# Output projection in token tiles of 512, 512, 64 and 512, 304, 272 in place of 364, 362, 362

## What is computed

```python
def _merge(att, h, mo, g_out, w_out):
    hl = _rmsnorm(jax.nn.sigmoid(mo) * h.astype(mo.dtype), g_out)
    lead = att.shape[:-1]
    mixed = jnp.concatenate([att.astype(hl.dtype), hl.reshape(lead + (LSTM_WIDTH,))], axis=-1)
    return mixed @ w_out
...
        xp = xp + _swiglu_half(xp, g_ffn1[l], w1_gate[l], w1_up[l], w1_down[l])
        dp, kp, vp, Cp, n_p, mp = _mix_prompt(xp, rows, *mix_w)
        xp = xp + dp
        xp = xp + _swiglu_half(xp, g_ffn2[l], w2_gate[l], w2_up[l], w2_down[l])
        xp = _rmsnorm(xp, g_final[l])
```

## Time and profile before

| | |
|---|---|
| Runs | 2407.89, 2411.44, 2412.19 us; median 2411.44 |
| Span of the profiled execution | 2406.2 us (its whole time isn't listed) |
| Mean granted clock of PE over the span | 0.961 |
| PE matmuls, weight loads | 2200.4 us (91%), 2126.2 us (88%) |
| DVE, ACT, POOL | 1016.1, 509.3, 155.5 us |
| HBM | 54 GB/s over the span |

### The profile page before, as it was taken

One profiled execution on the slowest core, in us unless ns is written; L12 is line 12 of the kernel. 1 busy time (PEld: TensorE's weight loads), 2 busy tenths in 40 slices (PEclk: granted clock), 3 DMA queues, 4 the chain that ended last, 5 costly groups with the idle time before them and its releaser, 6 DMA issues.

```text
span 2406.2 us, 32473 instructions
## 1 busy us (share of the span) xinstructions
PE 2200.4 (91%) x13110; PEld 2126.2 (88%) x13110; DVE 1016.1 (42%) x1699; ACT 509.3 (21%) x857; POOL 155.5 (6%) x216
## 2 busy tenths in 40 slices
PE   5999999999999978599994667999999999999997
PEld 4999999999999977488883656989999999999997
DVE  4533334343334365544433572263434333434335
ACT  3310011111011133333333451141111101111102
POOL 2100000000000010212220320010000000000000
PEclk8999999999999998799997887999999999999999
DMA  3301111101111012223220632102111011111002
GB/s 110 107 18 52 35 52 52 52 23 47 35 52 44 0 35 60 80 73 92 84 68 16 174 90 44 36 6 101 53 52 52 17 35 52 52 52 52 17 0 83
DMA packets 128003, 129.83 MB, mean 54 GB/s; under 512 B 10628, under 2 KB 115108, under 8 KB 127952
## 3 DMA queue, kind: packets, MB, share of 16 engines
q1 hardware_dynamic: 120224, 109.49, 15.3%
q0 software_dynamic: 7728, 19.65, 2.7%
HBM read 111.50 MB, written 17.55 MB: 54 GB/s over the span
## 4 chain that ended last, share of the span: by engine, by line
PE 51%; issue 34%; DVE 7%; ACT 5%; DMA 2%; POOL 1%; SPq 0%; DVEq 0%; ACTq 0%; POOLq 0%
PE bank L213 15%; PE bank L215 15%; PE bank L214 14%; PE bank L242 2%; ACT SP L843 1%; DVE RM L1121 1%; PE bank L1282 1%; PE bank L1272 1%; PE bank L1291 1%; DMA XIN<-in_x_prompt 1%; DVE SP L1056 1%; DVE WGL L308 1%; DVE YO L1182 0%; ACT L843 0%; DVE RS L248 0%
## 5 line engine op out<-in xcount | busy, mean ns | idle before, releaser
L213 PE MATMUL bank<-HH,WGH 128*128 128x362 f32 (+1 forms) x2856 | 948.4, 332 | 31.1 <-DVE WGL L308 13.2
L215 PE MATMUL bank<-HH,WGL 128*128 128x362 f32 (+1 forms) x2856 | 940.2, 329 | 0.0
L214 PE MATMUL bank<-HL,WGH 128*128 128x362 f32 (+1 forms) x2856 | 938.7, 329 | 0.0
L213 PEld LDWEIGHTS bank<-HH,WGH 128*128 128x128 f32 x2856 | 542.1, 190 | 42.6 <-issue 39.3
L214 PEld LDWEIGHTS bank<-HL,WGH 128*128 128x128 f32 x2856 | 542.3, 190 | 2.0 <-issue 0.5
L215 PEld LDWEIGHTS bank<-HH,WGL 128*128 128x128 f32 x2856 | 541.2, 189 | 0.0
L355 DVE TENSOR_TENSOR AT<-ST,bank 128x364 f32<-128x364 f32 (+1 forms) x132 | 70.2, 532 | 726.7 <-PE bank L215 726.7
L213 PE MATMUL bank<-AH,WDH 128*128 128x362 f32 (+1 forms) x1056 | 348.5, 330 | 9.8 <-DVE X L367 9.8
L215 PE MATMUL bank<-AH,WDL 128*128 128x362 f32 (+1 forms) x1056 | 346.6, 328 | 0.0
L214 PE MATMUL bank<-AL,WDH 128*128 128x362 f32 (+1 forms) x1056 | 345.4, 327 | 0.0
L367 DVE SCALAR_TENSOR_TENSOR X<-bank,X 128x362 f32<-128x362 f32 (+1 forms) x528 | 276.0, 533 | 154.0 <-PE bank L215 152.0
(11 more groups left out here) (221 smaller groups left out, 1460.7 us busy)
## 6 DMA issues: line engine op xcount, KB each, us to landing
RAWG<-in_w_gate SPq DMA_DIRECT2D x22, 1024.0 KB, 5.4
RAWU<-in_w_up SPq DMA_DIRECT2D x22, 1024.0 KB, 7.9
RAWD<-in_w_down SPq DMA_DIRECT2D x22, 1024.0 KB, 4.9
RAW<-in_w_in SPq DMA_DIRECT2D x22, 512.0 KB, 4.2
ZQ<-zm SPq DMA_DIRECT2D x8, 768.0 KB, 6.6
zm<-ZST POOLq DMA_DIRECT2D x32, 181.0 KB, 2.2
XIN<-in_x_prompt SPq DMA_DIRECT2D x2, 2048.0 KB, 13.8
RAW<-in_w_out SPq DMA_DIRECT2D x8, 512.0 KB, 9.1
```

What stands on the lines that cost most here:

```text
L213: nc.tensor.matmul(bank[:, 0:w], w_hi, rhs_hi, start=first, stop=False)
L214: nc.tensor.matmul(bank[:, 0:w], w_hi, rhs_lo, start=False, stop=False)
L215: return nc.tensor.matmul(bank[:, 0:w], w_lo, rhs_hi, start=False, stop=last)
```

## The change

A table `OUT_TILES` gives each batch of the output projection its own token tiles: 512, 512 and 64 columns for blocks 0 to 3, and 512, 304 and 272 for blocks 4 to 7. `unit_chain` takes the table as an argument, and DVE's addition takes its column range and width from it. Nothing else is changed: the same 24 chains of 24 matmuls, the same waits, and the same places of the norm's steps.

```diff
--- before.py
+++ after.py
@@ -36,6 +36,7 @@
 G0 = M0 + 4 * LH * LD
 UNITS = 23
 OUT_UNITS = KT
+OUT_TILES = [[(0, 512), (512, 512), (1024, 64)], [(0, 512), (512, 304), (816, 272)]]
 
 
 def wait_done(engine, semaphore, count):
@@ -459,8 +460,8 @@
 
             return (j - 4) // 4 + 1 if j % 4 == 0 else (j - j % 4) // 4 + 1 + (j % 4 == 1)
 
-        def unit_chain(pe, n, slot, bank):
-            t0, w = NTILE[n]
+        def unit_chain(pe, n, slot, bank, tiles=NTILE):
+            t0, w = tiles[n]
             for k in range(KT):
                 mm = three_pass(bank, w, WGH[:, slot, k], WGL[:, slot, k], HH[:, k, t0:t0 + w], HL[:, k, t0:t0 + w], k == 0, k == KT - 1)
             mm.then_inc(z.mm, 1)
@@ -1156,7 +1157,9 @@
                     for t in range(4):
                         q = 12 * batch + 4 * n + t
                         dve.wait_ge(z.mm, C1 + 48 + q + 1)
-                        nc.vector.tensor_tensor(x_view(4 * batch + t, n), x_view(4 * batch + t, n), BANK[q % 4][:, 0:NTILE[n][1]], ALU.add).then_inc(o_add, 1)
+                        t0, w = OUT_TILES[batch][n]
+                        x = X[:, 4 * batch + t, t0:t0 + w]
+                        nc.vector.tensor_tensor(x, x, BANK[q % 4][:, 0:w], ALU.add).then_inc(o_add, 1)
                         if n == 2 and batch == 0:
                             unit_low(dve, UNITS + 5 + t, t)
                         if n == 2 and batch == 1:
@@ -1388,7 +1391,7 @@
                     pe.wait_ge(z.lo, UNITS + 1 + 4 * batch + t)
                 if q >= 4:
                     pe.wait_ge(o_add, q - 3)
-                unit_chain(pe, n, t, BANK[q % 4])
+                unit_chain(pe, n, t, BANK[q % 4], OUT_TILES[batch])
                 if q == 19:
                     norm_pe(pe, norm[2], 0, BANK[4])
             pe.wait_ge(o_add, 3 * OUT_UNITS)
```

## The result

| | before | changed |
|---|---|---|
| Median of four runs | 2411.18 us | 2429.24 us |
| Lowest, highest | 2407.89, 2412.19 | 2425.13, 2432.62 |
| Span of the profiled execution | 2406.2 | 2423.6 |
| Mean granted clock | 0.961 | 0.956 |

The ratio is 1.0072 with a 95% interval of 1.0059 to 1.0084: slower by 17.4 us (14.2 to 20.3), which is the ratio times the median of before; the medians themselves are 18.1 us apart. The two profiled spans also differ by 17.4 us. The forecast was 2429.9 with a range of 2419 to 2437.

What follows compares the result with a forecast made beforehand. PE was taken to bound the projection, except its last stretch, set by DVE. Terms +7.4 (first blocks), +6.1 (clock), +3.9 (up to the norm), -0.4 and +1.5 (behind it) gave +18.5 us: 2429.9, range 2419 to 2437.

Steps and rivals of the forecast that it cites:

- Wide steps: Output projection matmuls at full clock: columns plus a surcharge, 15 ns fixed or proportional; middle 231.4 ns at 512 columns.
- the first blocks: Output projection, blocks 0 to 3: two 512-column steps and a narrow one replace 498 ns, +7.4 us at full clock.
- the chains ahead of the norm: Last four blocks before the first norm tile: 512 + 304 columns replace 364 + 362, +3.9 us.
- Narrow step: 64-column matmuls in blocks 0 to 3: weight load longer than the matmul, 112 ns at full clock.
- The upper bound from the mixed row counts: Narrow step, from the last mLSTM block's 64-column matmuls switching between 64 and 128 rows: 154 ns if all scales.
- Clock in the narrow stretch: 96 narrow matmuls in blocks 0 to 3 and wide work after: clock falls to half, together +6.1 us.
- Behind the norm: Last four 272-column chains: DVE's sequence sets the end, -0.4 us; PE's stop grows to 4.8 us, half clock costs +1.5.
- Rival (e): End of projection: DVE's end doesn't bind, 3.7 us come back, no stop or half clock; +13.7 us, chance 0.03.
- (a): Narrow stretch, blocks 0 to 3: the clock holds; total +12.4 us, 2424, chance 0.20.
- (b): Narrow steps: short matmuls don't overlap their loads, 154 ns full and 308 half clock; +28 us, 2440, chance 0.10.
- (c): Narrow steps: load hides as under transposes, 65 ns, clock falls late or not; +7.9 us, 2419, chance 0.08.
- (d): All projection steps: only columns at 2.4 GHz, surcharge belongs to something else; -2.4 us, 2409, chance 0.04.

Runs made afterwards that it cites:

- the second batch alone: Tiles 512, 304, 272 in blocks 4 to 7 only, blocks 0 to 3 as before, against the kernel before: 2416.85 against 2411.53 us, ratio 1.0022.

## Why the prediction was right

**Wide steps.** Forecast 231.4 ns for 512 columns, between a fixed and a proportional surcharge; measured 226.7. Over the columns at 2.4 GHz the surcharge is 13.4 ns at 512, 16 at 448 (4.86 us a chain), 13.3 at 384 (4.16), 12 at 420, 15 at 364, 11.2 at 304 and 10 at 272. It isn't proportional, but it isn't the fixed 15 ns either: at 512, 304 and 272 columns (226.7, 137.9 and 123.3 ns) the step lies below both bounds of the prediction. The middle was 4.7 ns too high at 512, which makes this the term with the largest error: the first blocks are 67.4 ns x 96 = 6.5 us dearer at full clock, not 7.4, and the chains ahead of the norm 3.2, not 3.9.

**Narrow step.** Forecast 112 ns, measured 112, and the tiles of 128 and 192 columns show that it doesn't depend on the columns. The upper bound from the mixed row counts doesn't apply here. That the floor is the weight load rests on the loads: in the narrow stretches their records fill the time (5.80 of 5.80 and 10.70 of 10.70 us), and behind a stop two loads are 0.11 us apart. No run takes the loads away. One reading of the prediction speaks for less than it seems to: the matmul records of its 128-column row don't last 107 ns but 0.39 us for two, so that only their distance of 112 ns counts. And its 64-column transposes, called ones with a shorter load, have loads of 128 columns too, though of 64 rows (timeline of PEld, before):

```profile
22.85 0.57 PEld L1198 LDWEIGHTS bank<-IDENT,XIN 64*128 64x128 f32 x8 [0.17 <-issue]
```

Eight such loads take 0.57 us. So the 112 ns hold for loads of 128 rows; whether fewer rows or the transposing makes the others quicker stays open. At half clock I took 190 ns, between the two loads behind a stop (164) and the 64-row matmuls (213); measured 213.

**Clock in the narrow stretch.** Forecast: a fall 4.4 us in, 57 steps at half clock, +4.4, and 3.7 us of wide work at half clock, +1.7. Measured: a fall after 6.1 us (2.8 in another kernel), 40 steps, +4.1, and 2.4 us lost in the chain behind. That is 6.5 against 6.1, and the closeness is luck: the fall came later than forecast, the half-clock step was longer, and more was lost behind the stretch. That the clock, and not the chains by themselves, costs this is shown by the kernel with the narrow chains between wide ones. How late the fall comes isn't settled: 6.1 and 2.8 us in two kernels whose code is the same up to there. With the fall of the second, the term would have been 9.6 us (69 steps, +7.0, and 2.6 behind), close to the upper end that the prediction gave it (about 10).

**Behind the norm.** Forecast -0.4 and a stop of 4.8 us; measured -0.4 and 4.99. Rival (e) is refuted by the second batch alone. The half clock behind the stop was to cost 1.5; it costs 1.4 to 1.6 in three traces and 2.3 to 2.8 in three others with the same second batch, as half clock lasts 3.4 or 6.8 us, in some of them beginning within the stop.

**The rivals.** (a), no fall, would have been +12.4; the kernel that removes the fall has +10.8 in its trace, and (a)'s excess over that lies in the steps of the wide tiles. (b) and (c) are refuted by 112 ns. (d) would have steps of 213.3 ns for 512 columns and 26.7 for 64; the traces have 226.7 and 112. The Trainium skill (TensorE: Matmul & The Clock Gate, section Back-to-back issue gap) gives columns at 2.4 GHz plus 2.5 ns for a warm matmul in isolation, by estimate 215.8 ns for 512 columns, and about 25 ns up to 64; for a stream with weight loads it has some 81 ns at 128 columns and 131 at 512. The traces of this float32r stream, 111.7 ns at 128 columns and 226.7 at 512, agree with neither. The same page of the Trainium skill, in its section on LDWEIGHTS, has a load take its columns over 1.2 ns, by estimate 107 ns for 128 columns; the step of 111.7 ns agrees, with some 5 ns on top. The transposes' loads of 128 columns and 64 rows, eight in 0.57 us, don't.

**The sum.** +18.5 was forecast, and the two stretches give +17.4: 6.5 + 6.5 + 3.2 - 0.4 + 1.55.

## What to carry to other kernels

With weights loaded for every matmul, narrowing a token tile saves time only down to a floor, and below it nothing (here 112 ns, by an estimate some 240 columns, from 112 ns less a surcharge of 11; 192 columns were at the floor, 272 above it). Filling a bank with 512 columns is worth nothing if it leaves a remainder of 64. A row of 64-column remainders can also drop PE to half clock while its records read as fully busy, so the granted clock has to be read beside the busy share. Where another engine's sequence sets the end of a stage, columns moved away from behind it are not saved but lead to a stop, and they are paid for where they are moved to.

## What the runs showed of the hardware that I had not expected

A float32r step at full clock costs its columns plus 10 to 16 ns at all widths from 272 to 512, with no clear growth (the 16 are at 448 columns), while at half clock there is nothing on top (364 columns in 0.30 us). The same width doesn't always cost the same: 304 columns from column 512 take 3.31 us a chain, from column 364 they take 3.36; and the kernel before takes 166.7 ns for 362 columns from column 726 in the first batch and 163.3 in the second. Why stays open.

At half clock the step of 64 columns is 213 ns, twice 107, although the first two loads behind a stop are only 0.16 us apart; the distance behind a stop is not the price in a stream.

Of six traces with the same stop of 4.99 or 5.00 us, three have half clock for 3.4 us and three for 6.8, and the restarts of the second three are 0.7 to 1.4 us longer.
